# The small tables of a top-16 choice, moved from SBUF into two PSUM accumulator banks

## The reference, cut to what matters

```python
def _peer(x, wq, k1, k2, u_tab, v_tab):
    q = (xt @ wq).reshape(T, PEER_HEADS, 2, PEER_DQ_HALF)
    s1 = jnp.einsum('thd,nd->thn', q[:, :, 0], k1)
    s2 = jnp.einsum('thd,nd->thn', q[:, :, 1], k2)
    v1, i1 = lax.top_k(s1, PEER_TOPK)
    v2, i2 = lax.top_k(s2, PEER_TOPK)
    cand = (v1[..., :, None] + v2[..., None, :]).reshape(...)
    cidx = (i1[..., :, None] * PEER_NKEYS + i2[..., None, :]).reshape(...)
    sc, pos = lax.top_k(cand, PEER_TOPK)
    eidx = jnp.take_along_axis(cidx, pos, axis=-1).reshape(T, PEER_HK)
    gate = jax.nn.softmax(sc.astype(jnp.float32), axis=-1)
    ...  # out = sum over chosen experts e of gate_e * gelu(u_e . x) * v_e
```

## Time and profile before

| | us |
|---|---|
| median of 3 runs | 3158.3 (3155.44 to 3162.97) |
| span of the profiled execution, first to last instruction | 3147.6 |
| PE busy in that span | 2982.5 |
| DVE, ACT, POOL busy | 2251.5, 1839.0, 1117.7 |

### The profile page before, as it was taken

One profiled execution on the slowest core, in us unless ns is written; L12 is line 12 of the kernel. 1 busy time (PEld: TensorE's weight loads), 2 busy tenths in 40 slices (PEclk: granted clock), 3 DMA queues, 4 the chain that ended last, 5 costly groups with the idle time before them and its releaser, 6 DMA issues.

```text
span 3147.6 us, 48399 instructions
## 1 busy us (share of the span) xinstructions
PE 2982.5 (95%) x17718; PEld 2613.9 (83%) x17718; DVE 2251.5 (72%) x3884; ACT 1839.0 (58%) x2813; POOL 1117.7 (36%) x1033
## 2 busy tenths in 40 slices
PE   7889999897999979898999999998989999999998
PEld 7768888776888857798999988887789999988887
DVE  5459999345899976598565487776579765557777
ACT  4658888444788855455555555555554555555554
POOL 3420000432000005688767501014569767620100
PEclk9989999998999989999999999999999999999999
DMA  5359999532899953465665677775346655677776
GB/s 205 114 189 350 374 370 370 182 141 86 303 374 369 365 187 118 134 188 192 191 185 181 211 248 238 245 239 183 128 135 213 186 189 180 186 237 245 240 243 205
DMA packets 203995, 701.76 MB, mean 223 GB/s; under 512 B 23602, under 2 KB 24754, under 8 KB 203504
## 3 DMA queue, kind: packets, MB, share of 16 engines
q1 hardware_dynamic: 170640, 619.07, 58.1%
q10 hardware_dynamic: 21056, 40.07, 3.5%
q0 software_dynamic: 12064, 39.52, 3.2%
HBM read 659.77 MB, written 38.80 MB: 222 GB/s over the span
## 4 chain that ended last, share of the span: by engine, by line
PE 87%; DVE 6%; POOL 3%; ACT 2%; DMA 1%; issue 1%; ACTq 0%; DVEq 0%; SPq 0%; POOLq 0%
PE ps L592 85%; POOL splitb L533 3%; PE ps L603 2%; DVE hrow L105 1%; DVE arena L95 1%; DVE arena L105 1%; ACT splitb L506 1%; DMA rawb<-in_peer_u 1%; DVE arena L100 0%; DVE hL L95 0%; DMA hrow<-in_x_rows 0%; ACT hH L159 0%; DMA spill<-gb 0%; ACT arena L159 0%; DMA rawb<-in_s_out 0%
## 5 line engine op out<-in xcount | busy, mean ns | idle before, releaser
L506 ACT ACTIVATE splitb<-rawb 128x512 fp32r<-128x512 f32 (+1 forms) x1306 | 826.7, 639 | 851.8 <-PE ps L592 708.4
L533 POOL TENSOR_TENSOR splitb<-rawb,splitb 128x512 fp32r<-128x512 f32 x571 | 775.3, 1374 | 855.9 <-ACT splitb L506 848.7
L592 PE MATMUL ps<-hH,splitb 128*128 128x256 f32 x5248 | 987.8, 287 | 18.8 <-POOL splitb L533 16.4
L592 PEld LDWEIGHTS ps<-hH,splitb 128*128 128x128 f32 x5248 | 836.9, 194 | 26.1 <-issue 14.3
L533 DVE TENSOR_TENSOR splitb<-rawb,splitb 128x512 fp32r<-128x512 f32 (+1 forms) x735 | 524.7, 733 | 409.1 <-ACT splitb L506 407.0
L592 PE MATMUL ps<-splitb,hid 128*128 128x512 f32 x3444 | 788.8, 389 | 2.6 <-ACT hid L159 2.6
L592 PEld LDWEIGHTS ps<-splitb,hid 128*128 128x128 f32 x3444 | 646.1, 188 | 138.4 <-ACT hid L159 3.4
L592 PE MATMUL ps<-hL,splitb 128*128 128x256 f32 x2624 | 747.2, 285 | 0.0
L592 PEld LDWEIGHTS ps<-hL,splitb 128*128 128x128 f32 x2624 | 508.4, 194 | 0.9 <-issue 0.5
L592 PE MATMUL ps<-experts_r 128*128 128x512 f32 (+2 forms) x1364 | 338.3, 397 | 16.5 <-ACT experts_r L159 9.0
L592 PEld LDWEIGHTS ps<-experts_r 128*128 128x128 f32 (+1 forms) x1364 | 256.6, 194 | 72.5 <-ACT experts_r L159 7.5
(11 more groups left out here) (163 smaller groups left out, 3320.2 us busy)
## 6 DMA issues: line engine op xcount, KB each, us to landing
rawb<-in_peer_u SPq DMA_DIRECT2D x256, 512.0 KB, 3.7
rawb<-in_peer_v SPq DMA_DIRECT2D x256, 512.0 KB, 4.2
experts<-in_moe_gu SPq DMA_DIRECT2D x228, 512.0 KB, 5.5
experts<-in_moe_d SPq DMA_DIRECT2D x108, 512.0 KB, 5.3
rawb<-in_moe_gu SPq DMA_DIRECT2D x92, 512.0 KB, 5.5
spill<-gb ACTq DMA_DIRECT2D x128, 256.0 KB, 4.2
aux<-spill POOLq DMA_DIRECT2D x128, 256.0 KB, 4.4
rawb<-in_moe_d SPq DMA_DIRECT2D x52, 512.0 KB, 5.5
```

Source lines behind the costliest of these rows:

```text
L506: self.eng.activation(S.split(m)[0], S.raw(n)[:, off:off + w], ACT.Copy).then_inc(S.hi.sem, S.hi.step(("half", m)))
L533: self.eng.tensor_tensor(l, raw, h.bitcast(F32), ALU.subtract).then_inc(self.low.sem, self.low.step(("half", m), *([("raw", n)] if last el ...
L592: return self.eng.matmul(o, w, x, start=start, stop=stop)
```

## The change

The tables `IIf` (indices as float), a new copy `V0` of the first side's values and `gs` (sums of the gates) lie in ps0; `PPf`, `PAf`, `PBf` (position, row, column) and one of the two working tables (`PY`) lie in ps1. The other working table, now `limit`, stays in SBUF. `dve_sides` names its working tables anew so that no operation has both tensors in one memory. One copy for each t is added.

```diff
-        self.IIf = R.get(16, 16)
         self.SC = R.get(8, 16)
         self.PP = R.get(8, 16)
-        self.PA = R.get(8, 16)
...
-        self.PPf = R.get(8, 16)
+        self.limit = R.get(8, 16)
...
-        self.gs = R.get(16)
+        first, second = S.accs[0], [S.accs[1][:, 128 * i:128 * i + 128] for i in range(4)]
+        self.IIf = first[:, 0:256].rearrange("p (a k) -> p a k", a=16)
+        self.V0 = first[:, 256:384].rearrange("p (h k) -> p h k", h=8)
+        self.gs = first[:, 384:400]
+        self.PPf, self.PY, self.PAf, self.PBf = (x.rearrange("p (h k) -> p h k", h=8) for x in second)
...
+        dve.cp(V0, v4[:, :, 0, :])
...
-            dve.tt(cand[:, :, at:at + w].rearrange("p h (a b) -> p h a b", b=width), bc(v4[:, :, 0, a0:a1], 3, width),
+            dve.tt(cand[:, :, at:at + w].rearrange("p h (a b) -> p h a b", b=width), bc(V0[:, :, a0:a1], 3, width),
                    bc(v4[:, :, 1, 0:width], 2, a1 - a0), ALU.add)
...
-        p, a, b, x, y = self.PPf, self.PAf, self.PBf, self.PA, self.PB
+        p, a, b, x, y = self.PPf, self.PAf, self.PBf, self.limit, self.PY
...
-        dve.stt(x, p, -48.4375, x, ALU.add, ALU.max)
-        dve.ts(x, x, 0.0, ROUND, ALU.max, ALU.add)
-        dve.ts(a, x, -ROUND, None, ALU.add, ALU.bypass)
-        dve.ts(x, a, 8.0, 8.0, ALU.mult, ALU.add)
-        dve.ts(y, a, 4.0, 24.0, ALU.mult, ALU.add)
+        dve.stt(y, p, -48.4375, x, ALU.add, ALU.max)
+        dve.ts(y, y, 0.0, ROUND, ALU.max, ALU.add)
+        dve.ts(a, y, -ROUND, None, ALU.add, ALU.bypass)
+        dve.ts(y, a, 8.0, 8.0, ALU.mult, ALU.add)
+        dve.ts(x, a, 4.0, 24.0, ALU.mult, ALU.add)
```

More of the change, by code:

```diff
@@ L2605, in __init__ @@
         self.II = [R.get(16, 16) for _ in range(2)]
-        self.IIf = R.get(16, 16)
         self.SC = R.get(8, 16)
         self.PP = R.get(8, 16)
-        self.PA = R.get(8, 16)
-        self.PB = R.get(8, 16)
-        self.PAf = R.get(8, 16)
-        self.PBf = R.get(8, 16)
-        self.PPf = R.get(8, 16)
+        self.limit = R.get(8, 16)
         self.oh = R.get(8, 16, 16)
         self.sel = [R.get(3, 128) for _ in range(2)]
-        self.gs = R.get(16)
+        first, second = S.accs[0], [S.accs[1][:, 128 * i:128 * i + 128] for i in range(4)]
[3 more added lines that the diff above has]
+        self.PPf, self.PY, self.PAf, self.PBf = (x.rearrange("p (h k) -> p h k", h=8) for x in second)
         self.kT2 = R.get(2, 128)
@@ L2831, in dve_choice @@
         iota16 = S.C["iota"][:, 0:16]
-        VV, II, IIf, SC, PP, oh, sel, gs = self.VV[t], self.II[t], self.IIf, self.SC, self.PP, self.oh, self.sel[t], self.gs
+        VV, II, IIf, V0, SC, PP, oh, sel = (self.VV[t], self.II[t], self.IIf, self.V0, self.SC, self.PP, self.oh,
+                                            self.sel[t])
         dve.cp(IIf, II.bitcast(U32))
```

## The result

| | us |
|---|---|
| kernel before, median of 6 runs | 3157.2 (3151.0 to 3163.0) |
| changed kernel, median of 6 runs | 3135.0 (3130.3 to 3139.7) |
| ratio, with its 95% interval | 0.9931 (0.9919 to 0.9943) |
| forecast | 3141.9, range 3137 to 3150 |
| spans of the two profiled executions | 3147.6 and 3131.2 |

The change makes the kernel faster, by 21.8 us in this comparison and by 18.6 us (0.9941, 0.9923 to 0.9958) in a second one. One launch of the kernel before in a later batch took 5254 us at a mean clock of 0.71 and is left out of its ratios.

The account below looks back on a forecast made before the run. PE was taken as the bound, waiting for POOL held by long DVE operations in both PEER layers. Four picking-stretch losses, 3.14 + 5.01 + 3.27 + 5.01 = 16.4 us, off 3158.3 gave 3141.9 us, range 3137 to 3150.

Parts of the forecast that it names:

- The mechanism: Both PEER layers: DVE operations with two SBUF tensors hold POOL, so its low halves take 2.30 us, not 1.29.
- The term that failed: PE's idle time in four index-picking stretches, two in each PEER layer, all regained: 16.4 us.
- The base: Time around the profiled span, 3158.3 - 3147.6 = 10.7 us, was said not to change.
- The range: 3137 to 3150 us: scatter 3139 to 3147, up to half the stall staying, 2 us lower for brief PE waits.
- Rival B: At ACT's table loads behind pairs 13 and 16, POOL starves: up to 0.8 us four times, 3145.1 us; chance 0.09.
- Rival C: In the picking, long operations still hold POOL: 3150 us if only index-table products do, 3158 if all; chance 0.07.
- Not more than 16.43 us: Upper bound on the gain, since no other PE wait for POOL lies in the two layers' windows.
- The trace agrees: 352 against 290 ns: Small 128-element DVE operations: a PSUM operand costs 0.06 us more than SBUF alone; the skill's rule says 65 ns.
- The rule of the Trainium skill on one SBUF input: A VectorE instruction with at most one SBUF input, outside two-port modes, does not contend with GpSimd.
- D: DVE's chain becomes the bound at ACT's exponential and PE's transposes in both layers: 3167.6 us; chance 0.04.
- the margin: DVE's choice ends 21 and 17 us before ACT needs the t = 1 exponents in the first and second layers.
- The cushion: The ring of split halves absorbs 2.1 us of POOL's 5.2 us shortfall in the first picking stretch.

Follow-up runs that it names:

- the fillers: The changed kernel with three or six more one-SBUF-tensor DVE reductions behind the picking of each t; ratios to the kernel before 0.9933 and 0.9969.
- the kernel with six reductions: The changed kernel with six more DVE reductions over the one-hot table for each t; ratio to the kernel before 0.9969 (0.9957 to 0.998).

## Why the prediction was wrong, and where it was right

The mechanism was right at each place where it could be tested: PE's loss was POOL's wait behind DVE's long operations with two SBUF tensors. One term of the sum was mis-sized.

- **The term that failed:** "The sum: 3.14 + 5.01 + 3.27 + 5.01 = 16.4 us off the span". These are the times in which PE is not busy, and they are less than what a stall costs. The timeline of PE in the kernel before shows why, at one stall (the last matmul ahead of it, and the first two behind):

```profile
1469.39 0.28 PE L592 MATMUL ps<-hH,splitb 128*128 128x256 f32 x1
1471.27 0.35 PE L592 MATMUL ps<-hH,splitb 128*128 128x256 f32 x1 [1.60 <-POOL splitb L533]
1471.47 0.28 PE L592 MATMUL ps<-hL,splitb 128*128 128x256 f32 x1
```

  The record of a matmul lasts 0.28 us, but unstalled the next one starts 0.12 us behind it. So the idle time begins 0.16 us late: from start to start the stall is 1471.27 - 1469.39 = 1.88 us, 1.76 more than the pace. And the matmul behind the stall is followed after 0.20 us and not 0.12, 0.08 more. This stall cost 1.84 us and is booked as 1.60. At all 14 stalls of the two layers the record ahead lasts 0.28 us and the matmul behind is followed after 0.19 to 0.20, so 14 x 0.24 = 3.4 us come on top of the 16.4: 19.8 us. The weight loads' row, idle 9.4 + 9.7 = 19.1 us in the two windows of before, comes nearer than PE's own.

  Counted in matmuls the same windows lose 20.0 us, of which 0.5 are left: 19.5. The forecast would have been 3158.3 - 19.5 = 3138.8, still above the 3135.0 measured. Of the 6.9 us between forecast and measurement this term is 3.1; the base is 1.1, since 3158.3 was the median of three runs and that of six is 3157.2; the other 2.7 stay open. The counts stood in the earlier trace rows: 121 matmuls in 18.10 us, where the pace of 241 in 28.62 gives 152. That is 31 x 0.119 = 3.7 us for the first stretch and not 3.14; the other three give 5.8, 3.8 and 5.8, in all 19.1.
- **The base.** "What lies around the span is 3158.3 - 3147.6 = 10.7 us" took the profiled execution for the median one. In the changed kernel's profiled run the whole took 3133.0 us and its span 3131.2: 1.8 us lie around it. So most of the 10.7 us was scatter between runs: 21 runs of before in the first batch had a median of 3154.4. The error does not reach the forecast, in which the 10.7 us cancel. The two spans differ by exactly the 16.4 us forecast, and this is chance: 19.4 us saved in the two stages, and 3 us more spent outside them, where the change does nothing. Over the nine traces this rest of the span goes from 2801 to 2811 us.
- **The range.** It allowed for a smaller gain (rivals B and C) and, for a larger one, no more than the scatter and 2 us. "Not more than 16.43 us" was stated as a bound, and it was none.
- **Right:** 2.29 us for the long operations with a PSUM tensor, as forecast. The small ones took 0.29 to 0.30 and not 0.352: DVE's choice ended at 1446.0 and was put at 1448.5. What a PSUM operand costs more than SBUF in a shape like this, 0.06 by the earlier trace rows and 65 ns by the Trainium skill (VectorE: DVE Perf Modes, section on the TRN2 errata), did not show. The rows with 0.352 have scalars from `arena` beside the PSUM tensor; the same operation on the same shape without them (`arena<-ps` at L100, eight times in the changed kernel) took 0.291. So "The trace agrees: 352 against 290 ns" compared two forms of operation, not two memories. The rule of the Trainium skill on one SBUF input (SBUF — State Buffer, section "Who interferes with whom") holds here at 2048 elements (2.29 us beside a busy POOL) and for copies into PSUM (0.29 us).
- **Rival B** did not come about: in the windows with ACT's loads and exponential PE was busy 100.00 and 99.85 of 100 us, and no wait for ACT or POOL is listed. **Rival C** is excluded by the rows of after, **D** by the margin, which the fillers measured: 3 x 2 reductions of 2.3 us, 13.8 us a layer, are free, twice as many are not.
- **The cushion** is there, since half of the holds cost far less than half, but its size, 2.1 us, was misread twice. The nine halves of the earlier trace rows count one that reaches over the edge; eight took 18.1 us, so a stretch of 18.1 us lacks 18.1 - 7.9 x 1.43 = 6.8 us and not 5.2. And PE lost 3.7 us there and not 3.14. That makes about 3.1 us, an estimate.

What stays open: 21.8 and 18.6 us are two estimates, good to about 4 and 5.5 us either way; the runs cannot tell 19.5 from 21.

## What to carry to other kernels

When an engine waits many short times, count its instructions against its unstalled pace in the same window, or measure a stall from start to start. Where records overlap, as PE's did here (0.28 us long, 0.12 us apart), idle time is less than what the waits cost, by 0.24 us for each stall. To free GpSimd it is enough to put one tensor of the long VectorE operations into PSUM: three tables gave the whole gain here, the rest gave nothing. VectorE's own time was worth nothing here up to a point: 14 us a layer could be given back free, and giving back 28 cost time. A profiled execution is one draw: take differences from it, and no offset to the median.

## What the runs showed that was not expected

- PE's waits of up to 1.62 us left the granted clock at 1.00 (2.4 GHz) in both traces of before. A wait of 2.97 us and one of 0.44 behind it, with 3 matmuls between, was followed by 4 us at 0.66, part of them at the lower level (1.2 GHz), in both layers of the kernel with six reductions. In the second layer the like window, 2454 to 2458, had 0.70.
- On VectorE, 128x128 operations from PSUM to PSUM took 0.30 us, from PSUM to SBUF or with one tensor of each 0.29: no dearer than the 0.29 of SBUF alone.
